# Sending an expert's weights in two halves of 1 MB, each when the half that stood in its place has been read

## What is computed

```
def expert_block(args):
    idx, e = args
    xb = x_pad[idx]
    hb = jax.nn.silu(xb @ w_gate[e]) * (xb @ w_up[e])
    return hb @ w_down[e]
```

## Time and profile before

| | us |
|---|---|
| median of 3 runs | 2027.74 (2023.86 to 2034.84) |
| the profiled execution's own time | 2025.0 |
| its span in the profile | 2023.2 |
| TensorE busy | 1937.7 (96% of the span) |
| VectorE busy | 753.2 |
| ScalarE busy | 435.8 |
| moved by the 16 DMA engines | 512.79 MB |

### The profile page before, as it was taken

One profiled execution on the slowest core, in us unless ns is written; L12 is line 12 of the kernel. 1 busy time (PEld: TensorE's weight loads), 2 busy tenths in 40 slices (PEclk: granted clock), 3 DMA queues, 4 the chain that ended last, 5 costly groups with the idle time before them and its releaser, 6 DMA issues.

```text
span 2023.2 us, 21323 instructions
## 1 busy us (share of the span) xinstructions
PE 1937.7 (96%) x8334; PEld 960.6 (47%) x8334; DVE 753.2 (37%) x1994; ACT 435.8 (22%) x886; POOL 86.3 (4%) x116
## 2 busy tenths in 40 slices
PE   7999999999999889999999999999988999999998
PEld 5444555444444335544455444444433464554555
DVE  3111354211111134345635322112114438875564
ACT  2001011011111015156311011111102532214454
POOL 0000000000000010022100000000001000000000
PEclk9999999999999999999999999999999999999999
DMA  7178179999999993211437999999999231220000
GB/s 287 42 151 313 63 295 393 429 426 429 429 428 428 425 368 151 83 54 71 176 150 319 406 428 428 428 428 428 427 426 375 84 116 42 83 84 1 12 11 22
DMA packets 46756, 512.79 MB, mean 253 GB/s; under 512 B 5297, under 2 KB 5425, under 8 KB 17329
## 3 DMA queue, kind: packets, MB, share of 16 engines
q1 hardware_dynamic: 38192, 481.38, 58.4%
q0 software_dynamic: 8448, 29.89, 3.8%
HBM read 484.90 MB, written 26.35 MB: 253 GB/s over the span
## 4 chain that ended last, share of the span: by engine, by line
PE 85%; DMA 6%; DVE 4%; ACT 2%; issue 2%; POOL 1%; SPq 0%; DVEq 0%; POOLq 0%; ACTq 0%
PE ps L948 21%; PE ps L987 10%; PE ps L489 8%; PE ps L921 8%; PE ps L1793 6%; PE ps L586 5%; PE ps L1347 5%; DMA ring<-in_wexp 4%; PE ps L1510 3%; PE ps L1991 3%; PE ps L2128 3%; PE ps L1541 2%; PE ps L1012 1%; PE ps L2165 1%; PE ps L2146 1%
## 5 line engine op out<-in xcount | busy, mean ns | idle before, releaser
L948 PE MATMUL ps<-ring,arena 128*48 128x512 f32 x1568 | 404.0, 605 | 37.8 <-issue 23.2
L948 PEld LDWEIGHTS ps<-ring,arena 128*48 128x48 f32 x1568 | 121.8, 125 | 238.9 <-issue 237.5
L961 DVE TENSOR_TENSOR arena<-arena,ps 48x512 f32<-48x512 f32 x64 | 44.2, 690 | 457.8 <-ACT arena L955 457.7
L987 PE MATMUL ps<-ring,arena 128*48 128x512 f32 x800 | 180.9, 592 | 1.1 <-ACT arena L975 1.1
L921 PEld LDWEIGHTS ps<-arena,h 128*128 128x128 f32 x1024 | 158.6, 190 | 44.6 <-issue 44.6
L921 PE MATMUL ps<-arena,h 128*128 128x192 f32 (+1 forms) x1024 | 174.3, 325 | 0.0
L489 PE MATMUL ps<-arena,ring 128*128 128x512 f32 x368 | 158.1, 592 | 0.0
L948 PE MATMUL ps<-arena 128*48 128x512 f32 x480 | 157.3, 602 | 0.9 <-issue 0.9
L955 ACT ACTIVATE arena<-ps 48x512 f32<-48x512 f32 x64 | 37.8, 590 | 471.7 <-PE ps L948 471.7
L1793 PE MATMUL ps<-ring,arena 128*128 128x512 f32 (+3 forms) x384 | 132.7, 500 | 0.8 <-DVE arena L364 0.8
L586 PE MATMUL ps<-ring,arena 128*128 128x512 f32 x256 | 114.6, 602 | 0.1
(11 more groups left out here) (285 smaller groups left out, 2082.4 us busy)
## 6 DMA issues: line engine op xcount, KB each, us to landing
ring<-in_wexp SPq DMA_DIRECT2D x148, 2048.0 KB, 19.1
arena<-in_wexp SPq DMA_DIRECT2D x44, 2048.0 KB, 21.6
ring<-in_wall SPq DMA_DIRECT2D x26, 2048.0 KB, 8.8
y_d<-arena POOLq DMA_DIRECT2D x60, 192.0 KB, 7.0
yo_d<-arena SPq DMA_DIRECT2D x2, 4032.0 KB, 41.9
xs_d<-h POOLq DMA_DIRECT2D x8, 512.0 KB, 4.4
ring<-in_wall SPq DMA_DIRECT2D x4, 1024.0 KB, 6.0
ring<-in_wall SPq DMA_DIRECT2D x2, 1536.0 KB, 6.6
```

What stands on the lines that cost most here:

```text
L948: mm = pe.matmul(outs[m], xeT[:, e_ // 4 % 2, k, e_ % 4 * CAP:(e_ % 4 + 1) * CAP], ws[m][:, k, :], start=(k == 0), stop=(k == KT - 1))
L961: dve.tensor_tensor(hh[0:CAP, e_ % 2, :], sl[0:CAP, e_ % 2, :], banks[1][64:64 + CAP, :], ALU.mult).then_inc(S["hh"], 1)
L987: mm = pe.matmul(outs[c], hT_of(e_ % 2)[:, k, :], w[:, k, c * 512:(c + 1) * 512], start=(k == 0), stop=(k == 3))
```

## The change

A layer's counts of `gu` and `dn` double: TensorE counts up in the middle and at the end of each gate/up product and of each down product, and everything that waits for them waits for the doubled value. SP sends an expert's unit with `sp_halves`: it waits until the first half of what stands in the place is read, issues 1 MB (8 KB a partition), waits until the second half is read, and issues the other 1 MB. Both count on the place's semaphore. For expert 31's down unit the first half counts on a semaphore of its own, `d_a`, and TensorE waits for the second half only ahead of step k = 2 of 4. Two semaphores of the router become one (`r_dif`). The loads of other stages still go through `sp_load`.

```diff
-        LAYER = dict(gu=NE, sl=NE, hh=NE, ht=NE, hTc=NE, dn=NE, ya=NE, yb=NE, xt=NE + 2, xtc=NE + 2, sel=NE // 4 + NT, pp=8, ppc=8, cmb=8, pg=8, pl_t=8, sg=8,
-                     ple_h=8, r_mm=4, r_lg=4, r_oh=4, r_cum=3, r_cnt=5, r_eg=1, r_exp=2, r_d2=1, hot=8, ixmm=1, ix=1, ovf=1, tw=1, tt=1, ttc=1, tmm=8, tadd=8,
+        LAYER = dict(gu=2 * NE, sl=NE, hh=NE, ht=NE, hTc=NE, dn=2 * NE, ya=NE, yb=NE, xt=NE + 2, xtc=NE + 2, sel=NE // 4 + NT, pp=8, ppc=8, cmb=8, pg=8, pl_t=8, sg=8,
+                     ple_h=8, r_mm=4, r_lg=4, r_oh=4, r_cum=3, r_cnt=5, r_dif=2, r_exp=2, d_a=16, hot=8, ixmm=1, ix=1, ovf=1, tw=1, tt=1, ttc=1, tmm=8, tadd=8,
...
-            loads = sum(1 for u in planned if u.slot == s and u.src is not None) + (src is not None)
-            u = Unit(s, SLOTS[s][:, 0:width], src, 16 * loads, freed, before)
+            loads = sum(u.parts for u in planned if u.slot == s)
+            u = Unit(s, SLOTS[s][:, 0:width], src, 0, freed, before)
+            u.parts = 0 if src is None else 2 if key[0] in ("gate", "up") or key[0] == "down" and key[2] < NE - 1 else 1
+            u.landed = 16 * (loads + u.parts)
...
-                plan(("gate", l, e_), t_["wexp"][l, e_, 0], UNIT, ("gu", NE * l + e_ + 1), slots=n_)
+                plan(("gate", l, e_), t_["wexp"][l, e_, 0], UNIT, ("gu", 2 * (NE * l + e_ + 1)), slots=n_)
...
+        def sp_halves(sp, key):
+
+            u = units[key]
+            half = UNIT // 2
+            for name, v in u.before:
+                sp.wait_ge(S[name], v - 1 if name in ("gu", "dn") else v)
+            first = (S["d_a"], 16) if u.parts == 1 else (S[f"ring{u.slot}"], 16)
+            sp.dma_start(u.ap[:, 0:half], u.src[:, 0:half]).then_inc(*first)
+            for name, v in u.before:
+                if name in ("gu", "dn"):
+                    sp.wait_ge(S[name], v)
+            sp.dma_start(u.ap[:, half:], u.src[:, half:]).then_inc(S[f"ring{u.slot}"], 16)
...
-            act.wait_ge(*M("r_eg", l, 1))
+            act.wait_ge(*M("r_dif", l, 1))
             act.activation(RT["eg"], RT["eg"], ACT.Exp).then_inc(S["r_exp"], 1)
-            act.wait_ge(*M("r_d2", l, 1))
+            act.wait_ge(*M("r_dif", l, 2))
...
@@ pe_gu
-            mm.then_inc(S["gu"], 1)
+                if k % 4 == 3:
+                    mm.then_inc(S["gu"], 1)
...
@@ pe_down
-            pe_unit(pe, ("down", l, e_))
+            if e_ == NE - 1:
+                pe.wait_ge(*M("d_a", l, 16))
+            else:
+                pe_unit(pe, ("down", l, e_))
             pe.wait_ge(*M("hTc", l, e_ + 1))
...
             for k in range(4):
+                if e_ == NE - 1 and k == 2:
+                    pe_unit(pe, ("down", l, e_))
                 for c in range(2):
                     mm = pe.matmul(outs[c], hT_of(e_ % 2)[:, k, :], w[:, k, c * 512:(c + 1) * 512], start=(k == 0), stop=(k == 3))
-            mm.then_inc(S["dn"], 1)
+                if k % 2 == 1:
+                    mm.then_inc(S["dn"], 1)
...
@@ act_down, dve_down (and act_gu, act_ht, dve_xt likewise)
-            act.wait_ge(*M("dn", l, e_ + 1))
+            act.wait_ge(*M("dn", l, 2 * e_ + 2))
...
@@ sp_moe
-                sp_load(sp, key)
+                sp_halves(sp, key)
```

More of the change, by code:

```diff
@@ L177, in plan_moe @@
                 n_ = RING + 2 if e_ <= 25 else RING
-                plan(("gate", l, e_), t_["wexp"][l, e_, 0], UNIT, ("gu", NE * l + e_ + 1), slots=n_)
-                plan(("up", l, e_), t_["wexp"][l, e_, 1], UNIT, ("gu", NE * l + e_ + 1), slots=n_)
+                plan(("gate", l, e_), t_["wexp"][l, e_, 0], UNIT, ("gu", 2 * (NE * l + e_ + 1)), slots=n_)
+                plan(("up", l, e_), t_["wexp"][l, e_, 1], UNIT, ("gu", 2 * (NE * l + e_ + 1)), slots=n_)
                 if e_ >= 1:
-                    plan(("down", l, e_ - 1), t_["wexp"][l, e_ - 1, 2], UNIT, ("dn", NE * l + e_), slots=n_)
-            plan(("down", l, NE - 1), t_["wexp"][l, NE - 1, 2], UNIT, ("dn", NE * l + NE))
+                    plan(("down", l, e_ - 1), t_["wexp"][l, e_ - 1, 2], UNIT, ("dn", 2 * (NE * l + e_)), slots=n_)
+            plan(("down", l, NE - 1), t_["wexp"][l, NE - 1, 2], UNIT, ("dn", 2 * (NE * l + NE)))
             spare_freed[l] = last[RING][1].freed + last[RING + 1][1].freed
@@ L755, in dve_router @@
             st = steps(dve)
-            dve.tensor_tensor(RT["eg"], lg[:, :, 0:4], RT["gm"].unsqueeze(2).broadcast_to([P, 4, 4]), ALU.subtract).then_inc(S["r_eg"], 1)
-            dve.tensor_tensor(RT["d2"], RT["m1"], RT["m0"], ALU.subtract).then_inc(S["r_d2"], 1)
+            dve.tensor_tensor(RT["eg"], lg[:, :, 0:4], RT["gm"].unsqueeze(2).broadcast_to([P, 4, 4]), ALU.subtract).then_inc(S["r_dif"], 1)
+            dve.tensor_tensor(RT["d2"], RT["m1"], RT["m0"], ALU.subtract).then_inc(S["r_dif"], 1)
             dve.wait_ge(*M("r_cnt", l, 5))
@@ L930, in dve_xt @@
             if p_ >= 2:
-                dve.wait_ge(*M("gu", l, 4 * (p_ - 2) + 4))
+                dve.wait_ge(*M("gu", l, 2 * (4 * (p_ - 2) + 4)))
             dve.tensor_tensor(xeT[:, p_ % 2, 2 * q_:2 * q_ + 2, z0:], banks[4 + t % 2][:, 0:8 * CAP].rearrange("p (k c) -> p k c", k=2)[:, :, z0:],
@@ L948, in pe_gu @@
                     mm = pe.matmul(outs[m], xeT[:, e_ // 4 % 2, k, e_ % 4 * CAP:(e_ % 4 + 1) * CAP], ws[m][:, k, :], start=(k == 0), stop=(k == KT - 1))
-            mm.then_inc(S["gu"], 1)
+                if k % 4 == 3:
+                    mm.then_inc(S["gu"], 1)
         def act_gu(act, l, e_):
-            act.wait_ge(*M("gu", l, e_ + 1))
+            act.wait_ge(*M("gu", l, 2 * e_ + 2))
             if e_ >= 2:
@@ L973, in act_ht @@
             if e_ >= 2:
-                act.wait_ge(*M("dn", l, e_ - 1))
+                act.wait_ge(*M("dn", l, 2 * e_ - 2))
             act.activation(hT_of(e_ % 2), banks[6][:, 0:4 * CAP].rearrange("p (k c) -> p k c", k=4), ACT.Copy).then_inc(S["hTc"], 1)
@@ L996, in dve_down @@
         def dve_down(dve, l, e_):
-            dve.wait_ge(*M("dn", l, e_ + 1))
+            dve.wait_ge(*M("dn", l, 2 * e_ + 2))
             if 2 <= e_ < NE - 1:
@@ L1049, in late @@
             def late(key):
-                return any(v > NE * l + OVF_AT + (name == "gu") for name, v in units[key].before if name in ("gu", "dn"))
+                return any(v > 2 * (NE * l + OVF_AT + (name == "gu")) for name, v in units[key].before if name in ("gu", "dn"))
             keys = []
```

## The result

The changed kernel takes 2039.72 us in the median of 7 executions (2034.63 to 2046.91), the kernel before 2028.65 (7 executions, 2023.86 to 2034.92). The ratio is 1.0041 with a 95% interval of 1.0022 to 1.0061: 4.5 to 12.4 us slower (the two medians are 11.1 us apart, the ratio stands for 8.3). The forecast was 2026.4, its range ended at 2034, and its side was wrong too. The profiled execution took 2038.7 us, span 2036.9.

A forecast was written before the change was run, and what follows sets the result against it. From about 336 us to each layer's end one unbroken stream of loads was taken to decide. Terms: -2 x 2.45 + 2 x 2.25 - 0.9 = -1.3 us, giving 2026.4 us against a median of 2027.74; range 2018.5 to 2034.

The forecast's parts named there:

- Part 1: Where the load queue runs dry, the first half of a freed unit goes early: 2.45 us gained a layer, ends 0 and 4.
- the lead is nothing: At the early issue, other traffic fills the gap and SP's order holds the rest: +3.6 us, 2031; chance 0.10.
- the lead is the whole advance: At the early issue, 4 us a layer, no cost of halves, store and gather 1.8: -9.8 us, 2018; chance 0.13.
- Once the queue is deep, an earlier issue is worth nothing: In the later loads, a unit that waits 25 us behind others lands when these are done: 0 gained.
- Part 2: Experts 7 to 31: 75 units a layer in halves at 0.03 us each, 2.25 us more a layer, ends 0 and 7.5.
- The finer-looking number: Cost of halves in the stream, from 2.364 against 2.351 us a MB: 0.03 us a unit, rounding allowing 0 to 0.05.
- the coarser one: Cost of halves from two ple halves landing 2.4 us apart: from no loss up to 0.1 us more a unit.
- Rival 1: In both layers' streams, 150 added transfers cost more: slower from 0.039 us each, +5.4 us at 0.075, 2033; chance 0.22.
- a full rate of 425 GB/s or less: Sign in the full slices of the loads: 426 to 428 GB/s was forecast, 425 or less would point to rival 1.
- Part 4: SP's doubled issues, TensorE's counts in mid product and the router's single semaphore all cost nothing.
- the last product: Expert 31's down product waits for ScalarE's copy, not its weights, so beginning with half of them gains 0.
- Part 3: End of a layer: layer 0's chain passes a store that gains 0.9 us, ends 0 and 1.8; layer 1 gains 0.

The follow-up runs named there:

- e2: The kernel before, each unit stored as two blocks of 1 MB and read by one transfer with rows of 8 KB; 2041.34 us, ratio 1.0063.
- e8: The changed kernel, but each unit in four transfers of 512 KB (4 KB rows), sent when the whole place is read; 2063.95 us, 1.0168 of the kernel before.
- e1: The changed kernel without the early issue: both halves sent when the whole place is read; 2041.34 us, 1.0045 of the kernel before.
- e4: The changed kernel, halves only up to expert 7 and for the last down unit, other units whole; 2025.58 us, 0.9979 of the kernel before.
- e5: The kernel before, whole units recut: first holds steps 0 to 3 of gate and up, second steps 4 to 7; 2021.00 us, ratio 0.9955.
- e10: The changed kernel with only the doubled counts and expert 31's down unit in halves, all other units whole; ratio 0.9998 to the kernel before.
- e9: The kernel before, each expert's unit as two 1 MB transfers over even and odd partitions, rows of 16 KB; ratio 1.0005.
- e3: The kernel before, each expert's unit as two 1 MB transfers, partitions 0 to 63 and 64 to 127, rows of 16 KB; 2782.48 us, ratio 1.3617.
- e7: The changed kernel, halves only up to expert 7, both freed units' first halves sent in mid gate/up product; 2026.36 us, 0.9974 of the kernel before.

## Why the prediction was wrong

**What bounds the kernel: right.** The loads' stream from about expert 6 on sets the start of expert 31's product; e2 and e8 slow that stream alone, by 5.3 and by 17.5 and 16.6 us, and the stretch from 1 to 31 grows by 5.5 and 5.6, and by 19.0 and 16.7.

**Part 1, the lead: right in place and size.** 2.45 us a layer forecast, 2.2 and 2.3 measured (e1 against the changed kernel), 2.1 and 1.3 as a gain over the kernel before (e4). Of the two rivals on it, "the lead is nothing" falls, and "the lead is the whole advance" too: the landings of the changed kernel are 2.8 and 2.9 us early at the first unit and 1.8 and 2.3 at expert 7's. "Once the queue is deep, an earlier issue is worth nothing" held: e4 drops it there and loses nothing.

**Part 2, "I take 0.03, because it is the same stream in the same form": the step that failed.** A unit in halves costs 0.069 us more, not 0.03: 5.2 us for 75 units instead of 2.25, more than the lead. The text said that the rounding of 1.25 MB allowed 0 to 0.05. The truth lies outside that bound. Part of it is the rounding: the window's 168 packets are 152 rows of 8 KB and 16 semaphore writes, 1.245 MB, so it is 2.372 us a MB and 0.046 us a unit, all of the bound. The rest is that "the same stream in the same form" didn't hold: a row of 8 KB took 310 ns in the mean in that window, in which only the two halves were on their way, and 313 in the changed kernel's experts (500 to 540 us), where many are queued. The stores between them aren't the reason: rows more than 2 us away from any packet of another queue took 313 too. What makes the 3 ns stays open. The finer-looking number was put in place of the coarser one, whose end of 0.1 held the truth. The trace of before held a better price, which the expectation of e8 names: the typical row took 611 ns at 16 KB and 309 at 8 KB, 7 ns more for two short ones, on 8 added rows an engine 0.056 us a unit. With 0.069 in its place the sum is 150 x 0.069 - 5.8 = +4.6 us, 2032: the forecast's side turns. By the landings the price is 0.076, and the sum +5.6.

**The rest, some 6 us of the median's 11 or 4 of the ratio's 8, had no term.** In the traces: the stretches of the changed kernel are 5.1 + 3.4 = 8.4 us longer (before rounding), and the landings at expert 31's up unit account for 3.7 + 3.1 = 6.8. The other 1.6, nearly all in layer 0, isn't in the stream. The 2.2 us ahead of expert 0 and the 2.0 between experts 0 and 1 are mostly the clock at the start of the stage (0.4 us of the 2.2 is there at 27 us, long before any expert). e1 and e5 show the same clock, 0.66 from 256 to 276 us, and the start of expert 0 at 270.0 and 269.8 us, e5 being faster than the kernel before; e2, e4, e10 and e8 start it at 268.0, 267.1, 266.7 and 266.2. So it doesn't belong to the halves, as far as these profiles can tell. The prediction allowed 1.7 us for the clock; this one pair of profiles has about 4.

**Rival 1 was the right one, with 0.22.** It named the place (added transfers in the stream) and its point of decision, 0.039 us; what it had wrong is the carrier: not a transfer's end but a row's. By the prediction's own sign, a full rate of 425 GB/s or less, the run points to this rival. Of the Trainium skill's page "DMA: Bandwidth & Descriptors", what speaks against 1 MB transfers is the measured table in the section Bandwidth (341 GB/s at 1 MB, for transfers issued from GpSimd). The section Rules for kernel authors asks for 1 MiB or more a transfer, which the halves meet. The table would have put the loss on the size of the transfers. e9 disagrees for a queue that is full: 1 MB transfers at 428 GB/s.

**Part 4 and the last product: right.** The last product's split 0 (e10), counts in the middle 0 (e10).

**Part 3, the store: the duration right, the path wrong.** The store takes a median of 5.9 us for 7.0 on the page, 1.1 less where 0.9 was worked out; e8, with 4 KB rows, has 5.4. But that is bought by the slower stream (in e4, with long rows, it is 7.0 again), and in layer 0, where the sum counted it, the chain that ended last no longer has a store in it. It goes by expert 31's product, which takes 8.77 us there, and both last down products:

```profile
733.44 8.77 PE ps L963 x32
742.21 3.45 PE ps L1008 x16
...
746.58 3.65 PE ps L1008 x16
```

So the 0.9 us were not earned there. In layer 1 it is the other way round: the chain before had no store, the one after has (5.84 us). "Layer 0 by the store, layer 1 not" was no property of the kernel: e4 and e10 have no store in the chain of layer 0 either.

## What to carry to other kernels

Where a queue of loads is never empty, only its rate and its head start count: send early at the points where the queue runs dry, and leave the transfers' shape alone elsewhere. If a finer release is wanted, cut the data so that what is read together lies together at full row length (e5), rather than cutting rows in two. And price a change of 1% by a plateau of the rate, never by the quotient of two rounded numbers, one of them from a few transfers that stood alone.

## What the runs showed of the hardware

- A row (the contiguous run that one partition gets) costs about 9 ns on its engine beyond its bytes: 428, 422 and 410 GB/s with rows of 16, 8 and 4 KB, the same bytes and a full queue. The rows' own mean durations from 500 to 540 us, 615, 313 and 163 ns (before, changed, e8), would make it 11 to 12 ns; why the two differ wasn't looked for. The Trainium skill's page "DMA: Bandwidth & Descriptors" (Specifications) asks for no more than 512 B for line rate. These runs differ from that by 1.4% at 8 KB and 4.2% at 4 KB, which decides where the loads are the bound.
- Loads of 64 adjacent partitions each, queued one behind the other, ran at 212 to 237 GB/s; the same loads over even and odd partitions at 428 (e3, e9). The cause was not looked for.
- TensorE's clock was granted low (1.2 instead of 2.4 GHz) for more of the gate/up products where the rows are short to the end: those that took over 8 us, expert 0's left out, are 9 to 12 in both layers of such a kernel (10 in the changed one, 11 in e1, 9 in e2, 12 in e8), and 4 or 5 with long rows at the end (4 before and in e4, 5 in e7, e9 and e10). What the engine did before differs by little: ahead of expert 26's slow product it was idle for 1.66 us, ahead of the same product before, which took 7.07, for 1.43, and its waits in that part of layer 0 add up to 16.8 us, before 16.5. Why the clock fell more often stays open. At expert 26 it is hidden, since the next product starts 15.34 us later, at the pace of the loads; at expert 31 (8.77 us in layer 0 after, in layer 1 before) nothing hides it. Between executions of the changed kernel the time goes with the clock: 2034.63 us at a mean of 0.986, 2046.91 at 0.976.
